# VectorE's place for the weights of a pair of experts: before or after a step of the next head's choices

## The reference

```
q = (xb @ w_pq).reshape(t, PEER_HEADS, 2, PEER_HALF)
s = einsum('thpd,phkd->thpk', q, keys)
top_s, top_i = top_k(s, 16)                       # of both halves
best_s, best_j = top_k(all 16 x 16 sums, 16)
expert = take_along_axis(cand_i, best_j)          # 16 of 16384 experts
g = softmax(best_s)
h = einsum('td,thkd->thk', xb, u_emb[expert])
act = g * gelu(h)
out = einsum('thk,thkd->td', act, v_emb[expert])
```

## Time and profile before

| | |
|---|---|
| median of 3 runs | 3593.12 us (3592.84 to 3595.46) |
| the profiled execution | 3593.41 us, span 3591.7 us |
| busy share of the span | PE 71%, PEld 30%, DVE 68%, ACT 28%, POOL 40% |
| gathers (queue 0) | 1140.92 MB of 1220.43 MB, 9.0 us from issue to landing |
| mean rate | 340 GB/s over the span |

### The profile page before, as it was taken

One profiled execution on the slowest core, in us unless ns is written; L12 is line 12 of the kernel. 1 busy time (PEld: TensorE's weight loads), 2 busy tenths in 40 slices (PEclk: granted clock), 3 DMA queues, 4 the chain that ended last, 5 costly groups with the idle time before them and its releaser, 6 DMA issues. The chain is left out here.

```text
span 3591.7 us, 41643 instructions
## 1 busy us (share of the span) xinstructions
PE 2535.7 (71%) x13407; PEld 1076.0 (30%) x13407; DVE 2442.1 (68%) x6857; ACT 1020.4 (28%) x2925; POOL 1418.8 (40%) x1266
## 2 busy tenths in 40 slices
PE   5999867666866677667666866687667666666654
PEld 3444533222322233223322332233223222222211
DVE  2888666667666666776667667666667666666774
ACT  2333322222222222222322222323332222222321
POOL 0332434434444443444434443434344434344443
PEclk9999889887888898888888988887888878888866
DMA  7112369999999999999999999999999999999997
GB/s 251 47 50 70 98 230 381 382 386 383 396 391 384 380 386 379 380 379 385 393 380 382 388 379 388 374 385 376 385 370 401 378 374 369 344 385 371 365 371 297
DMA packets 219401, 1220.43 MB, mean 340 GB/s; under 512 B 33091, under 2 KB 60419, under 8 KB 79942
## 3 DMA queue, kind: packets, MB, share of 16 engines
q0 software_dynamic: 156672, 1140.92, 81.4%
q1 hardware_dynamic: 62533, 77.09, 6.6%
HBM read 1199.51 MB, written 18.42 MB: 339 GB/s over the span
## 5 line engine op out<-in xcount | busy, mean ns | idle before, releaser
L1374 PE MATMUL ps<-uv_rows,diag 64*64 64x512 f32 x8704 | 1381.8, 761 | 967.7 <-ACT diag L1619 966.8
L1270 POOL DMA_INDIRECT uv_rows<-in_uv_emb,experts x1088 | 1255.6, 1154 | 1823.9 <-PE ps L1374 1536.1
L1832 DVE CUSTOM_DVE_ANT_0 uv_rows<-uv_rows,handed 128x1024 f32<-128x1024 f32 x1088 | 1331.9, 1224 | 862.6 <-DMA uv_rows<-in_uv_emb,experts 856.7
L1374 PEld LDWEIGHTS ps<-uv_rows,diag 64*64 64x64 f32 x8704 | 329.1, 157 | 1655.0 <-ACT diag L1619 1221.8
L1611 ACT ACTIVATE gelu_c<-dots 128x2 f32<-128x2 f32 x544 | 110.8, 204 | 1880.4 <-DVE dots L1832 1880.0
L1619 ACT ACTIVATE diag<-ident_twice,act_c 128x64 f32<-128x64 f32 x1088 | 319.1, 340 | 286.4 <-DVE act_c L1849 285.8
L1334 PE MATMUL ps<-w_pq_sb,xnT_c 128*128 128x256 f32 x1152 | 349.1, 434 | 0.7 <-ACT xnT_c L1580 0.7
L1334 PEld LDWEIGHTS ps<-w_pq_sb,xnT_c 128*128 128x128 f32 x1152 | 224.7, 212 | 260.6 <-issue 236.0
L568 PE MATMUL ps<-w_in_sb,w_out_sb 128*128 128x512 f32 (+1 forms) x656 | 243.3, 526 | 16.8 <-ACT w_out_sb L454 16.8
L626 DVE SCALAR_TENSOR_TENSOR handed<-w_out_sb,tapsT,handed 128x128 f32<-128x128 f32 x960 | 252.8, 343 | 0.0
L389 POOL TENSOR_TENSOR rstd_a<-ms_a,neg_half 128x1 f32<-128x1 f32 x9 | 82.5, 9166 | 205.2 <-ACT ms_a L435 205.2
(11 more groups left out here) (244 smaller groups left out, 2127.1 us busy)
## 6 DMA issues: line engine op xcount, KB each, us to landing
uv_rows<-in_uv_emb,experts POOLq DMA_INDIRECT x1088, 9.0
w_in_sb<-in_w_in SPq DMA_DIRECT2D x4, 2048.0 KB, 11.7
w_pq_sb<-in_w_pq SPq DMA_DIRECT2D x8, 1024.0 KB, 12.2
w_out_sb<-in_x_prompt SPq DMA_DIRECT2D x8, 512.0 KB, 3.9
handed<-in_x_prompt SPq DMA_DIRECT2D x8, 512.0 KB, 3.8
w_out_sb<-in_w_out SPq DMA_DIRECT2D x1, 4096.0 KB, 19.3
out<-handed SPq DMA_DIRECT2D x8, 512.0 KB, 9.3
keys_turned<-handed SPq DMA_DIRECT2D x10, 260.0 KB
```

The source lines that it names most:

```text
L1270: nc.gpsimd.indirect_dma_start(out=rows[:, m % RING, :], out_offset=None, in_=d.uv_emb[0], in_offset=bass.IndirectOffsetOnAxis(ap=experts[ ...
L1374: ins = pe.matmul(ps[dst, 2 * x + half, :], diag[src, (m + i) % DIAGS, :], rows[src, (m + i) % RING, cols], start=first, stop=last)
L1832: nc.vector.tensor_tensor_reduce(out=row, in0=row, in1=xn[:, block_of(n) % 2, :], scale=1.0, scalar=0.0, op0=ALU.mult, op1=ALU.add, accum_ ...
```

## The change

In the loop of VectorE, the call of `weights` for a pair moves from behind the step (or steps) of the choices at the second dot of the pair to ahead of it, right behind the dot. In the first head after a block it thereby also moves ahead of the first half of `add_residual`, at k = 1. Nothing else changes.

```diff
@@ -2004,6 +2004,8 @@
                 ends = n >= PH and n % PH == 0
                 for k in range(K):
                     dot(n, k)
+                    if k % GROUP == GROUP - 1:
+                        weights(n, k // GROUP)
                     if len(steps) == 1 and ends:
 
                         for _ in range(0 if k < 4 or k == 5 else 1 if k < 12 else 2):
@@ -2015,8 +2017,6 @@
                         next(steps[k // (K // 2)], None)
                     if ends and k == 1:
                         add_residual(block_of(n) - 1, 0)
-                    if k % GROUP == GROUP - 1:
-                        weights(n, k // GROUP)
                     if ends and k == 1:
                         add_residual(block_of(n) - 1, 1)
                     if ends and k == 3:
```

## The result

The changed kernel took 3550.86 us (median of 4 runs, 3533.39 to 3562.92) against 3594.29 (4 runs, 3592.84 to 3607.65): 43 us less. The ratio of the means is 0.9867, 95% interval 0.982 to 0.9915. So the change is worth some 43 to 53 us. I had forecast 16 us, 3577, with a range from 3556 to 3600: the sign was right, the size about a third.

What follows compares the result with a forecast made beforehand. It took the expert stage to be bound by DMA transfers, with 69 us idle. From 3593.4 us it subtracted 15, 1 and 3 and added 2.5, giving 3577 us, range 3556 to 3600.

Steps and rivals of the forecast that it cites:

- Where the delay sits, and how long it is: Second dot's sum to end of weights: 1.18 us becomes 0.50; VectorE's wait there about 140 us in place of 45.
- The first pair: Each head's first pair: weights 0.68 us earlier; 15 us gained in ordinary heads, bounds nothing and 23.
- The dry windows: Fourth to sixth dot of a head, where DMA engines run dry: share to rise from 0.91 to nearer 0.95.
- the heads with two choices: First pair in four heads with two choices, at 0.3 us each: 1 us gained.
- The other pairs: Pairs after a head's first: 3 us gained, bounds nothing and 27 us.
- ceiling of 69 us: Idle DMA time in the expert stage, 58 plus 11 us: the most VectorE could give back without shortening transfers.
- the seven windows: Fourth to sixth dot in seven ordinary heads: DMA idle time 3.46 us in all, 0.49 a head.
- The rule set against the change: Expert stage, DMA busy 0.98: by the skill's rule reordering VectorE is worth nothing, time 3593.4 us.
- No change: Idle time in the first pair's window is unevenness between DMA engines: 3587 to 3599, centre 3592; chance 0.20.
- Slower: Third and fourth dots of each head: VectorE's standstill delays the second pair by 0.27 us; 3611 us, chance 0.10.
- Much faster: First pair's matmuls: higher TensorE clock releases it up to 1.8 us earlier still; about 3552 us, chance 0.08.
- The block's first head: First pair there: residual sum waits for the weights, release 0.31 us later; 2.5 us lost, bounds nothing and 11.

Runs made afterwards that it cites:

- e1: Kernel before, with the weights moved ahead of the step only at each head's first pair (k = 1): ratio 0.9943 to the kernel before.
- e2: Kernel before, with the weights moved ahead of the step at all pairs but each head's first: ratio 0.9931 to the kernel before.
- e0: The changed kernel measured once more, no edit: ratio 0.9852 to the kernel before.
- e4: Changed kernel plus an unused VectorE reciprocal ahead of each pair's weights, to delay them: ratio 1.0061 to the kernel before.
- e5: Changed kernel with eight row buffers instead of six, and query weights of four heads used twice: 3379.05 us, ratio 0.9366 to the kernel before.
- e6: Kernel before (weights behind the step) with eight row buffers and query weights of four heads used twice: 3380.02 us, ratio 0.937.
- e10: Changed kernel with both diagonals of a pair formed by VectorE right after the gelu, none by ScalarE: 3528.22 us, ratio 0.9788 to the kernel before.

## Why the prediction was wrong in size

*Where the delay sits, and how long it is.* Right. The weights come 0.49 us after the sum at the median, the step follows, and VectorE waits 130 us for the gelu in all, where I had written 140.

*The first pair.* Right in the place, small in the size. The dry windows closed as forecast. The terms that e1 covers were 15 us, 1 for the heads with two choices and 2.5 lost in the blocks' first heads, 13.5 together; e1 measured 20 (15 to 26), close to the upper end of 23 that I had cut to two thirds.

*The other pairs.* Here the prediction failed: 3 us, measured 25 (15 to 35) in e2. The step at fault is the sentence that "a pair's round is late only where the DMA engines run dry", and with it the ceiling of 69 us read off the busy share. Eight buffers took 173 us out of the same stage. The share counts an engine as busy while its packet is on the way, however slowly. The earlier trace rows had it side by side: before the late issue 1.00 and 418 GB/s, after it 0.69 and 213. By the share 31% of those 2 us were lost, by the rate 49%, and a busy engine moved 213/0.69 = 309 GB/s instead of 418. Had I read the loss of the seven windows by their rates against 418, it would have been 7.1 us instead of 3.5, and that of the stage 2902 x (1 - 380/418) = 264 us instead of 58.

*What sets the pace instead.* With six buffers the round does: delays of 0.07 to 0.4 us a pair on the mean, up and down, were worth 0.27 to 0.54 of themselves (e0, e1, e2, e4), where three pairs in a ring give a third, and the landing time stayed at 8.9 to 9.1 us. Timed in the traces for pairs 40 to 499, the round, from a pair's first gather to the one that takes over its buffer, was 17.01 us before and 16.74 in e0. The way from the sum to the second diagonal gave 0.22 of that; from the first issue to the landing of the second row it was 11.19 us before and 11.12 in e0 (11.27 in the slower profile after). With eight buffers the transfers do, and the place of the weights is worth nothing (e5, e6): that part of the round is 15.50 us in e6 and 15.76 in e5, so it grew by 0.26 where the diagonals came 0.22 sooner. That the round binds is shown, the exact third is not: the measured worth lies on either side of it. That packets on a starved engine are slow is read from rates and not tried by itself.

*The rule set against the change.* The Trainium skill, Perfetto Trace Analysis, section What "DMA-bound" means, was applied to a kernel that was not yet so bound. At six buffers, with 0.98 of busy time and 380 GB/s, the conclusion that I drew from it, that VectorE's order is worth nothing, did not hold; at eight, with 407 GB/s, it did.

*The rivals.* No change is out. Slower is out: dots wait less for rows than before, but 715.6 us over 1088 is still 0.66 us each, so VectorE's standstill stayed covered. Much faster had the right time, 3552, by the wrong way, so its agreement is luck: TensorE's matmuls take 761 ns on the mean after as before. At the first pairs the clock gave some 0.2 us (3.33 against 3.10), not 1.8, and the other pairs lost as much.

*The block's first head.* 0.28 us later where I had 0.31.

## What to carry to other kernels

A ring of buffers can bind while the transfer engines look busy: compare the rate in its best windows with the rate of the stage before believing a busy share, and look whether the landing time grows when gathers are issued sooner. While the ring binds, a microsecond less in a stage of every round is worth about one over the number of pairs in the ring (here 0.15 to 0.54 for a third, more where the transfers had run dry), so in-order engines should do the ring's own work ahead of anything with slack. Two more buffers showed at once, even in a kernel that leaves something out, where the bound of the transfers lies.

## What was not expected of the hardware

The DMA share hardly moved over kernels that differ by 6% in time: 0.98 at 380 GB/s, 1.01 at 407. Matmuls of 64 x 64 quarters ordered by row did not release the first row early: sixteen still took 1.96 us, and the first release came only 0.09 us before the last. Two VectorE instructions over 128 x 64 numbers with two scalars per partition take 0.54 us one behind the other (e10).
